# Mixers of a one-core block kernel: pooling sums and the halved mean on VectorE, rotated heads on 128 rows, convolution norm ahead of the gates, new order on three engines

## The reference, cut to what matters

```python
z = h @ w_in
xp, ca, cg, q, k, v, g = jnp.split(z, splits, axis=-1)      # 256, 256, 256, 4 x 512
y_pool = pool_mixer(xp, pool_w, pool_scale)
y_conv = conv_module(ca, cg, conv_dw, conv_db, conv_ln_g, conv_ln_b, conv_pw)
y_ret = retention(q, k, v, g, ret_gn_g)
mix = jnp.concatenate([y_pool, y_conv, y_ret], axis=-1) @ w_out
h = layer_norm(DEEPNORM_ALPHA * h + mix, ln_g[l, 1], ln_b[l, 1])
```

## Time and profile before

| what | value |
|---|---|
| median of three runs | 2303.89 us (2303.3 to 2304.95) |
| the profiled execution | 2299.75 us |
| its span in the trace | 2297.9 us |
| granted TensorE clock, mean over the span | 0.972 |
| TensorE (PE) busy in the span | 2194.2 us |
| VectorE (DVE) busy | 1605.1 us |
| ScalarE (ACT) busy | 1041.6 us |
| GpSimd (POOL) busy | 210.4 us |

### The profile page before, as it was taken

The page is one execution under the profiler, slowest core; times in us unless marked ns, Lnnn a source line. Parts: engine busy times, 40 slices in busy tenths (PEclk is TensorE's granted clock), DMA queues, the critical chain, the costliest instruction groups (busy, mean ns, idle before and its releaser), DMA issues. The chain is left out here.

```text
span 2297.9 us, 35725 instructions
## 1 busy us (share of the span) xinstructions
PE 2194.2 (95%) x15008; PEld 2007.0 (87%) x15008; DVE 1605.1 (70%) x2406; ACT 1041.6 (45%) x1513; POOL 210.4 (9%) x219
## 2 busy tenths in 40 slices
PE   6999998999999999899999998999999997997997
PEld 6999978999999997899998776798888886587997
DVE  5878896978887887797852467576445337757775
ACT  5433534433544353544443345535444324755662
POOL 2100232100210032210000001000000000100000
PEclk9999999999999998999998999999999998998999
DMA  5665524667466552476622121023222222113553
GB/s 211 238 224 202 195 74 178 235 221 257 185 228 222 194 184 74 184 275 226 216 87 75 38 73 62 20 74 111 92 102 100 92 75 91 37 46 115 184 175 106
DMA packets 47487, 331.75 MB, mean 144 GB/s; under 512 B 5532, under 2 KB 6652, under 8 KB 8288
## 3 DMA queue, kind: packets, MB, share of 16 engines
q1 hardware_dynamic: 37808, 266.35, 32.8%
q0 software_dynamic: 9520, 63.11, 7.1%
HBM read 328.40 MB, written 1.05 MB: 143 GB/s over the span
## 5 line engine op out<-in xcount | busy, mean ns | idle before, releaser
L2005 DVE TENSOR_TENSOR WLO<-RAW,WHI 128x2048 fp32r<-128x2048 f32 x252 | 583.6, 2317 | 257.7 <-ACT WHI L1453 254.7
L459 PE MATMUL PS<-XB,WHI 128*128 128x256 f32 (+1 forms) x3072 | 701.5, 324 | 16.7 <-DVE XB L2353 12.4
L1453 ACT CAST WHI<-RAW 128x2048 fp32r<-128x2048 f32 x252 | 476.1, 1892 | 312.3 <-DMA RAW<-in_dn_c 78.1
L459 PEld LDWEIGHTS PS<-XB,WHI 128*128 128x128 f32 x3072 | 518.0, 192 | 63.6 <-issue 19.1
L459 PE MATMUL PS<-XHI,WHI 128*128 128x272 f32 (+1 forms) x1760 | 513.4, 294 | 18.7 <-ACT XHI L1461 15.1
L459 PE MATMUL PS<-XHI,WLO 128*128 128x272 f32 (+1 forms) x1760 | 508.2, 291 | 0.0
L459 PE MATMUL PS<-XB,WLO 128*128 128x256 f32 (+1 forms) x1536 | 494.2, 322 | 0.0
L459 PE MATMUL PS<-XLO,WHI 128*128 128x272 f32 (+1 forms) x1760 | 486.1, 290 | 0.0
L459 PEld LDWEIGHTS PS<-XHI,WHI 128*128 128x128 f32 x1760 | 339.5, 193 | 24.2 <-issue 18.9
L459 PEld LDWEIGHTS PS<-XHI,WLO 128*128 128x128 f32 x1760 | 339.1, 193 | 0.0
L459 PEld LDWEIGHTS PS<-XLO,WHI 128*128 128x128 f32 x1760 | 328.2, 192 | 0.4
(11 more groups left out here) (363 smaller groups left out, 2713.2 us busy)
## 6 DMA issues: line engine op xcount, KB each, us to landing
AW<-in_ada POOLq DMA_DIRECT2D x48, 1024.0 KB, 7.2
RAW<-in_up_c SPq DMA_DIRECT2D x44, 1024.0 KB, 4.9
RAW<-in_up_a SPq DMA_DIRECT2D x42, 1024.0 KB, 4.9
RAW<-in_up_b SPq DMA_DIRECT2D x42, 1024.0 KB, 4.9
RAW<-in_mix SPq DMA_DIRECT2D x30, 1024.0 KB, 4.9
RAW<-in_dn_a SPq DMA_DIRECT2D x22, 1024.0 KB, 4.9
RAW<-in_dn_b SPq DMA_DIRECT2D x22, 1024.0 KB, 4.9
RAW<-in_dn_c SPq DMA_DIRECT2D x22, 1024.0 KB, 4.9
```

Source lines behind the costliest of these rows:

```text
L459: return pe.matmul(o, w, x, start=first, stop=last)
L1453: act.copy(WHI1[:, s, 0:w], RAW[:, s, 0:w]).then_inc(w1_high, 1)
L2005: v.tensor_tensor(WLO1[:, s, 0:w], RAW[:, s, 0:w], WHI1[:, s, 0:w].bitcast(F32), ALU.subtract)\
```

## The change

**Pooling and shift.** The nine pooling instructions move from POOL to VectorE (`pool_windows`), between taps 24 to 28 and `decay(2)`; so do the four subtractions of `shift_x` (`shift(c)`), two after `rest(u0 + 13)` and two behind XLO1. POOL gets two memsets instead, of the third blocks of V1 and ST.

**Heads.** `rotate(n)` now adds in place into T1, and ScalarE's `place_rotated(n)` copies it in four pieces of 64 partitions, so that QK[:, h] is one head on 128 partitions. `scores(h)` takes one matmul of 128 rows per block of keys, `values(h)` takes 128 rows for the third block too. `rotated` is now raised by ScalarE, and `rotate(n)` waits for it before it writes T1 again.

**Order.** TensorE runs `values(0)` before unit u0+8, the convolution's mean, scores(3), values(2) and the variance one behind the other ahead of the gate unit u0+10, and the pooling product after `values(3)`. VectorE takes more taps early (4 instead of 2 before the first rotation), `rest` of u0+8 and u0+9 later, and the convolution norm ahead of `head_gain(0)`. ScalarE follows.

```diff
@@ gpsimd, mixer @@
+                pool.memset(V1[:, 2, :], 0.0).then_inc(pads_set, 1)
+                pool.memset(ST[:, :, 2, :], 0.0).then_inc(pads_set, 1)
                 add_halves(q)
-                pool.wait_ge(rotated, 4 * l + 4)
-                shift_x(q)
...
@@ tensor, mixer @@
                 def scores(h):
+                    pe.wait_ge(rotated, 4 * l + 3 + h // 2)
                     if h == 0:
-                        pe.wait_ge(rotated, 4 * l + 4)
+                        pe.wait_ge(rot_step, 8 * l + 8)
...
-                        for a in range(2):
-                            last = mm(pe, PS[0:w, 4 + jt, 0:L1], QK[q64, 4 + 2 * (h // 2) + a, jt * P:jt * P + w],
-                                      QK[q64, 2 * (h // 2) + a, :], a == 0, a == 1)
+                        last = mm(pe, PS[0:w, 4 + jt, 0:L1], QK[:, 4 + h, jt * P:jt * P + w], QK[:, h, :], True, True)
...
@@ scalar, mixer @@
+                def place_rotated(n):
+
+                    act.wait_ge(rot_sum, 4 * l + n + 1)
+                    for h in range(2):
+                        for a in range(2):
+                            last = act.copy(QK[64 * a:64 * a + 64, 2 * n + h, :], T1[64 * h:64 * h + 64, a, :])
+                    last.then_inc(rotated, 1)
...
@@ vector, mixer @@
-                    v.tensor_tensor(QK[:, 2 * n:2 * n + 2, :], T1[:, :, :], T2[:, :, :], ALU.add).then_inc(rotated, 1)
+                    v.tensor_tensor(T1[:, :, :], T1[:, :, :], T2[:, :, :], ALU.add).then_inc(rot_sum, 1)
...
+                def shift(c):
+
+                    tk = tokens(q)
+                    v.wait_ge(half_copied, q + 1)
+                    v.wait_ge(rotated, 4 * l + 4)
+                    v.tensor_tensor(pair(c, tk), XL[:, 2 * c:2 * c + 2, tk], bc(MH[:, tk], 2), ALU.subtract)\
+                        .then_inc(x_shifted, 1)
```

More of the change, by code:

```diff
@@ L887, in mixer @@
                 unit(u0 + 9, 2, XHI1, XLO1).then_inc(unit1_done, 1)
-                pe.wait_ge(pool_step, POOL_STEPS * (l + 1))
+                pe.wait_ge(conv_tap, 62 * (l + 1))
                 pe.wait_ge(xp_copied, l + 1)
[L890 to L896, removed]
                 for t in range(2):
@@ L899, in mixer @@
                 last.then_inc(cv_mean, 1)
-                pe.wait_ge(w1_split, u0 + 11)
-                pe.wait_ge(gs_done, 2 * l + 1)
-                unit_tile(u0 + 10, 0, 2, XHI1, XLO1)
+                scores(3)
+                values(2)
                 pe.wait_ge(cv_squared, l + 1)
@@ L906, in mixer @@
                 last.then_inc(cv_var, 1)
+                pe.wait_ge(w1_split, u0 + 11)
+                pe.wait_ge(gs_done, 2 * l + 1)
+                unit_tile(u0 + 10, 0, 2, XHI1, XLO1)
                 values(3)
+                pe.wait_ge(pool_step, POOL_STEPS * (l + 1))
+                pe.wait_ge(cv_centred, l + 1)
+                pe.wait_ge(cv_std, l + 1)
+                for t in range(2):
+                    last = mm(pe, PS[:, t, 0:L1], PW[:, t, :], PM[:, t, :], True, True)
+                last.then_inc(pooled, 1)
                 unit_tile(u0 + 10, 1, 3, XHI1, XLO1).then_inc(unit1_done, 1)
@@ L2241, in centre_values, with pool_windows @@
                     last.then_inc(v_centred, 1)
+                def shift(c):
[4 more added lines that the diff above has]
+                        .then_inc(x_shifted, 1)
+                def pool_windows():
+                    v.wait_ge(xp_copied, l + 1)
+                    v.wait_ge(pads_set, 8 * (l + 1))
+                    v.wait_ge(tab1_loaded, 16 * 6 * (l + 1))
+                    st = Steps(v, pool_step, POOL_STEPS * l, POOL_STEPS)
+                    src, n = XP, 16 + L1
+                    for j in range(4):
+                        w = 1 << j
+                        lo = 2 * w - 1
+                        st.link(v.tensor_tensor(PT_[j][:, :, lo:n], src[:, :, lo:n], src[:, :, lo - w:n - w], ALU.add))
+                        src = PT_[j]
+                    for j in range(4):
+                        q64 = slice(64 * (j % 2), 64 * (j % 2) + 64)
+                        st.did(v.tensor_tensor(WN[q64, j // 2, :], PT_[j][q64, j // 2, 16:n], IC[q64, j // 2, :],
+                                               ALU.mult))
+                    st.wait()
+                    st.did(v.tensor_tensor(PM[:, :, :], WN[:, :, :], XP[:, :, 16:n], ALU.subtract))
+                    st.end()
                 def head_gain(h):
@@ L2293, in mixer @@
                 rest(u0 + 13)
[L2294 to L2298, removed]
+                shift(0)
+                shift(1)
                 head_gain(2)
@@ L2306, in mixer @@
                         .then_inc(y_low, 1)
+                shift(2)
+                shift(3)
                 for h in range(RH + 1):
```

96 lines of the change are left out of this document (44 added, 52 removed).

## The result

The changed kernel takes 2279.55 us, median of four runs (2273.05 to 2285.14), beside 2303.94 for the kernel before (four runs, 2303.3 to 2304.95): a ratio of 0.9893, 95% interval 0.9864 to 0.9921. Forecast was 2282. The profiled execution took 2277.08 us, its span is 2275.2, 22.7 less than before's.

The account below looks back on a forecast made before the run. TensorE, busy 95% of the span, was taken as the bound, with its clock and a full VectorE in the first mixer's middle. Scores 12.2, clock 11.9 and removed waits 3.1, less 1.2, 2.3 and 1.7, gave 22.0: 2282 us, range 2274 to 2295.

Parts of the forecast that it names:

- The scores: TensorE's scores calls: six 128-row records replace twelve of 64, 3.04 us becomes about 1.5; eight calls save 12.2 us.
- POOL's work on VectorE: VectorE per layer: 9.3 us of tap slowing by POOL goes, 7.8 us of pooling and shift work comes.
- The waits: TensorE in the mixers: ST waits removed, 3.1 us; new tap waits add 1.2 us, longer XLO1 waits 2.3 us.
- 315.4: VectorE's list, first mixer: time at which pooling ends, after taking 5.2 us.
- six taps 318.9: VectorE's list, first mixer: last six taps end at 318.9; TensorE wants them at 318.3, waiting some 0.6 us.
- 310.2: VectorE's list, first mixer: eight taps end at 310.2, then pooling begins.
- The clock: TensorE in both mixers: two long 1.2 GHz stretches go, saving 5.1 + 6.8 = 11.9 us.
- the two reasons: Why the long 1.2 GHz stretches go: the waits they begin at go, and matmuls of 64 and 16 rows become 128.
- One fall of 1.7 us: Clock at the new XLO1 wait before dense fp32r matmuls: one fall over the two layers, costing 1.7 us.
- Sum: Whole kernel: 12.2 + 11.9 + 3.1 - 1.2 - 2.3 - 1.7 = 22.0 us faster.
- VectorE becomes the bound: Rival, chance 0.05: taps stay slow without POOL, TensorE waits 10 us per layer; about 1.5 us faster, 2302.
- The clock stays a problem: Rival, chance 0.13: clock falls for long at the new waits, 11.9 us do not come; 10 us faster, 2294.

Follow-up runs that it names:

- heads alone: Kernel before with only the new 128-row scores and ScalarE copies; old order, pooling and shift on POOL: 2304.99 us beside 2304.67, ratio 1.0.
- order alone: Kernel before with only the new order on the three engines; heads on 64 rows, pooling and shift on POOL: 2287.78 us, ratio 0.9912.
- heads undone: Changed kernel with heads back on 64 rows, no ScalarE copies; new order kept, pooling and shift on VectorE: 2296.09 us, ratio 0.9962.
- all shifts late: All four shifts behind XLO1's write: on the changed kernel 2278.78 us, 0.9885; on it with heads back on 64 rows 2290.26 us, 0.9923.
- second profile: Changed kernel run again unaltered, to see its spread: 2281.27 us (2274.44 to 2285.3), ratio 0.9880.
- order + heads: Changed kernel with pooling and shift back on POOL, also spelled "both back"; new order and 128-row heads kept: 2286.62 us, ratio 0.9922.
- rearrangement: Changed kernel, last taps ahead of pooling sums, XLO1 ahead of reciprocal, gains and shifts, head's spread earlier on TensorE: 2270.14 us, ratio 0.9838.

## Why the prediction was right, and where its sizes were off

**The scores.** Right: the step from one group to the next is 1.57 us, where 1.52 was taken off 3.04. That gives 8 x 1.47 = 11.8 us instead of 12.2. What the prediction didn't see is on what this term hangs. It stands in the sum as if it came by itself. The runs say: alone 0, on top of the order 0, on top of the order with POOL's work on VectorE 0.9962 - 0.9893 = 0.7%, 16 us, and with all shifts late on both sides 0.9923 - 0.9885 = 0.4%, 9 us. The last pair is the cleanest, since its waits for XLO1 are equal: 11.8 us less work, less 3.1 us of new waits for the taps, is 8.7. On top of the order, with POOL's work on POOL, the new waits for the taps are 6.6 us, and up to 5.1 us go at the clock's falls beside them: together 11.7 of the 11.8. A saving on TensorE arrives only as far as the taps and the decayed scores are early enough.

**POOL's work on VectorE.** Right in kind, since the taps all run at 0.42 us. In size: pooling took 5.6 us, not 5.2, and copies 1.7 a group, not 1.5, with waits of up to 0.94 us behind them on VectorE.

**The waits.** ST's went, as said. For the taps the forecast had 0.6 us and there were 1.5 and 1.6: the step that failed is "315.4" for the end of the pooling, and with it "six taps 318.9". TensorE's scores(0) began 2 us earlier than before, where the clock's stretch at the mixer's start was shorter (0.83 from 240 to 250 instead of 0.70), which nothing in the change explains. Less these 2 us, TensorE stood at the taps' wait 0.4 us earlier than forecast (317.42 - 1.54 = 315.9, against 316.3). VectorE kept the 2 us up to the pooling (308.22 where the list had 310.2), so the copies cost it next to nothing; pooling took 0.4 us of them, and the taps ended at 317.4, against 316.9. The two make the 0.9 us. For XLO1 2.1 was forecast, 2.4 measured. Together the waits took 2.5 us more than the forecast had.

**The clock.** Right that both long stretches would go. Of the two reasons, rows alone are ruled out by the run with heads undone; that it is the waits and nothing else is not shown. The rule of the Trainium skill, "TensorE: Matmul & The Clock Gate", section "What's actually happening", by which the clock follows how busy TensorE is and says nothing of rows, agrees with that run (64 rows, no wait, 1.00). It does not say why 0.51 us of waiting stood ahead of 10 us at 1.2 GHz before and 1.5 us ahead of none in the changed kernel. "One fall of 1.7 us" was a mean that neither profile of the changed kernel had: none in the first, three in the second, of which two behind XLO1's wait.

**Sum.** By the profiled executions 22.7 us against 22.0. That this is so near is in part luck. Against the forecast there are 2 us of luck at the start of the first mixer, no fall at the new waits (1.7 better), and 3 us lost by the larger waits and the 11.8. These three alone give 22.7, but two more lie beside them that cancel: some 4.5 us won up to the second XLO1 that the terms don't hold, and 4.3 us lost behind it. To XLO1 the first mixer won 348.90 - 337.43 = 11.5, or 9.5 without that luck, where 9.8 was forecast; up to the second mixer's XLO1 it is 917.29 - 890.26 = 27.0, where 23.4 was. Of the 3.6 us more, 2 are that luck, and 1.5 came between the first XLO1 and the stage behind the mixer, where a wait of 1.07 us for POOL's sums (at 375.21 before) is gone. The 4.3 us that are lost again behind it lie where the change touches nothing. In the slices of 2 us, two places there have 27 us at 1.2 GHz (from 1120 and from 1208) where before had 17 (from 1150 and from 1234); half of the difference is 5 us. That fits, but what moves those stretches was not tried.

**The rivals.** "VectorE becomes the bound" was refuted for the changed kernel, but it is the state in which heads alone and order + heads are. "The clock stays a problem" exists in small: the second profile has a fall behind XLO1's wait in each mixer, 3.4 us each, which lose 1.7 us each; behind the waits for the taps neither profile has one.

## What to carry to other kernels

A saving on the busiest engine must be paid out by the engine that feeds it: before counting it, put both lists side by side at the next place where they meet, with the saving in, and ask who is late there. Count a removed wait together with the clock that falls behind it; where a queue is full, first move what is waited for ahead of what is not, which gave more here (20 us by the medians for the order alone, 9 to 11 for the rearrangement) than making TensorE's work smaller did by itself.

## What the runs showed of the hardware that was not expected

- A blocked POOL can wait very long: one subtraction of 128x272 took 9.64 us beside sixteen taps, where the median of its kind took 0.79. One addition of 128x574 took 5.51 us with both back, in which VectorE finished a `rest` and eight taps at their usual pace, and the same addition took 1.27 us in the order alone, where VectorE was for the most part waiting for TensorE.
- The clock did not fall in one profile and fell in the next at the same waits of 2.4 us, to the tenth. Runs of one kernel spread by 12 us. The two profiles differ by 18 us in their time at 1.2 GHz, of which at most half is lost, and by 4.2 us in their span. Taking 2.5 us of waits for XLO1 away was worth 6 us with the heads undone and nothing that could be told in the changed kernel.
- The length of a wait does not say whether the clock falls behind it: after 0.51 us among small 64-row fp32 products it averaged 0.68 over 16 us, after 1.5 and 1.6 us ahead of small 128-row fp32 products it stayed at 1.00 in both profiles of the changed kernel, and after 1.1 and 1.2 us ahead of dense output blocks there was no fall in either mixer of the order alone. What decides is not shown.
